# A product of zeros on TensorE ahead of each expert row of the last three tiles

## What is computed

```python
def expert_block(args):
    xi, ii, gi = args                              # 128 tokens, 128 experts each
    h = jnp.einsum('nhkd,nd->nhk', peer_u[ii], xi)
    a = jax.nn.gelu(h.astype(f32), approximate=False) * gi
    return jnp.einsum('nhk,nhkd->nd', a.astype(x.dtype), peer_v[ii])
```

## Time and profile before

| what | value |
|---|---|
| median of 3 runs | 2049.05 us |
| the profiled execution's own time | 2053.64 us |
| its span, first to last instruction | 2051.8 us |
| TensorE matmul busy, share of the span | 1600.6 us, 78% |
| GpSimd busy | 1224.8 us, 60% |
| VectorE busy | 1245.5 us, 61% |
| mean granted TensorE clock | 0.864 of full |
| moved by DMA | 675.08 MB, mean 329 GB/s |

### The profile page before, as it was taken

How to read it: one execution, slowest core, us unless ns; L and a number is a source line. 1 busy time by engine, 2 the same in 40 slices (tenths; PEclk the granted TensorE clock), 3 DMA queues, 4 the chain that set the end, 5 groups by cost and what they waited for, 6 DMA issues and landing times.

```text
span 2051.8 us, 16855 instructions
## 1 busy us (share of the span) xinstructions
PE 1600.6 (78%) x4837; PEld 798.0 (39%) x4837; DVE 1245.5 (61%) x3135; ACT 440.0 (21%) x1035; POOL 1224.8 (60%) x1370
## 2 busy tenths in 40 slices
PE   7988888879989897963758777758777757676867
PEld 6787464445444432411323323223332323222323
DVE  7821459878697776677857664455666436443534
ACT  2342112452333213111111111110212111111111
POOL 0181057755776666676666666666766665666663
PEclk9988989989999999986868798778887878778978
DMA  5453389987999999899899999999999998999996
GB/s 215 139 153 94 127 339 363 345 321 267 379 368 379 408 374 387 304 361 349 338 364 366 360 364 380 350 373 369 372 360 357 378 379 322 367 372 352 377 360 230
DMA packets 186699, 675.08 MB, mean 329 GB/s; under 512 B 20976, under 2 KB 23456, under 8 KB 186192
## 3 DMA queue, kind: packets, MB, share of 16 engines
q0 software_dynamic: 167056, 609.25, 78.6%
q1 hardware_dynamic: 17632, 59.51, 8.2%
q10 hardware_dynamic: 1920, 5.24, 0.7%
HBM read 669.71 MB, written 3.69 MB: 328 GB/s over the span
## 4 chain that ended last, share of the span: by engine, by line
PE 58%; issue 18%; DVE 10%; POOL 6%; DMA 5%; ACT 2%; another core or an unknown queue 2%; SPq 0%; DVEq 0%; ACTq 0%; POOLq 0%
PE bank L1035 40%; PE bank L930 2%; POOL region L693 2%; POOL region L680 2%; DMA wring<-in_pu,region 2%; PE first_banks L930 1%; PE bank L838 1%; DVE region L1510 1%; PE bank L734 1%; DMA small<-in_pv,region 1%; DVE region L1498 1%; DMA discretisation<-in_pv,region 1%; PE first_banks L987 1%; PE bank L987 1%
## 5 line engine op out<-in xcount | busy, mean ns | idle before, releaser
L1035 PE MATMUL bank<-region,small 128*128 128x512 f32 (+1 forms) x728 | 379.5, 658 | 124.7 <-issue 61.6
L693 POOL DMA_INDIRECT region<-in_pv,region x320 | 326.8, 1021 | 190.2 <-issue 80.8
L680 POOL DMA_INDIRECT region<-in_pu,region x298 | 310.2, 1041 | 162.2 <-issue 83.8
L1510 DVE CUSTOM_DVE_ANT_0 wring<-wring,first_banks 128x1024 f32<-128x1024 f32 x228 | 271.9, 1217 | 144.8 <-DMA wring<-in_pu,region 83.0
L680 POOL DMA_INDIRECT wring<-in_pu,region x278 | 270.2, 972 | 124.8 <-issue 77.1
L1035 PEld LDWEIGHTS bank<-region,small 128*128 128x128 f32 (+1 forms) x728 | 140.6, 198 | 337.3 <-issue 281.0
L1510 DVE CUSTOM_DVE_ANT_0 region<-region,first_banks 128x1024 f32<-128x1024 f32 x156 | 187.2, 1218 | 91.3 <-DMA region<-in_pu,region 66.8
L1035 PE MATMUL bank<-region 128*128 128x512 f32 x364 | 187.1, 648 | 54.8 <-issue 51.4
L1510 DVE CUSTOM_DVE_ANT_0 region<-region 128x1024 f32<-128x1024 f32 x142 | 171.7, 1224 | 45.0 <-DMA region<-in_pu,region 39.0
L1801 ACT ACTIVATE small<-small,region 128x128 f32<-128x128 f32 (+1 forms) x317 | 105.2, 385 | 314.7 <-issue 108.8
L1809 ACT ACTIVATE region<-region 128x4 f32<-128x4 f32 x144 | 29.3, 203 | 523.0 <-DVE region L1510 302.6
(11 more groups left out here) (371 smaller groups left out, 2410.9 us busy)
## 6 DMA issues: line engine op xcount, KB each, us to landing
wring<-in_w SPq DMA_DIRECT2D x100, 512.0 KB, 5.5
region<-in_pv,region POOLq DMA_INDIRECT x320
region<-in_pu,region POOLq DMA_INDIRECT x298
wring<-in_pu,region POOLq DMA_INDIRECT x278
region<-in_w SPq DMA_DIRECT2D x4, 512.0 KB, 4.9
small<-in_small ACTq DMA_DIRECT2D x1, 1669.0 KB, 9.0
xT<-in_xT SPq DMA_DIRECT2D x1, 1536.0 KB, 12.7
region<-in_x SPq DMA_DIRECT2D x3, 512.0 KB
```

The source lines that it names most:

```text
L680: pool.indirect_dma_start(ring_u[u_at.place[q]], None, io["pu"], bass.IndirectOffsetOnAxis(ind[:, k:k + 1], 0)).then_inc(g_u[u_at.place[q] ...
L693: pool.indirect_dma_start(ring_v[v_at.place[q]], None, io["pv"], bass.IndirectOffsetOnAxis(ind[:, k:k + 1], 0)).then_inc(g_v[v_at.place[q] ...
L1035: last = mm(bank[6 + hf][0:tn, :], diagonal[diag_at[d]][:, 0:tn], ring_v[v_at.place[q]][:, 512 * hf:512 * hf + 512], start=k == 0, stop=t ...
L1510: V.tensor_tensor_reduce(out=ring_u[u_at.place[q]], in0=ring_u[u_at.place[q]], in1=first_banks[:, :] if t > 1 else x1[t], scale=1.0, scala ...
```

## The change

In `weigh`, for every slot of the last three tiles but a tile's first, TensorE first adds the product of a 128x128 matrix of zeros with 256 columns of a constant to the sums in bank 6. It stands ahead of the waits for the slot's diagonal and for its V rows. The zeros are written once by ScalarE, in `do_banks(2)`, in the room of the sixteenth diagonal, so that the ring of diagonals shrinks from 16 to 15.

```diff
-DIAGS, LATE_DIAGS = 8, 16
+DIAGS, LATE_DIAGS = 8, 15
...
+        zeros = view(12928, 128)
...
+                    if t > 1 and k:
+                        if q == slot_base[2] + 1:
+                            pe.wait_ge(zeros_s, 1)
+                        mm(bank[6][0:tn, 0:256], zeros[:, 0:tn], s("k12")[:, 0:256], start=False, stop=False)
                     d = q - by_dve[q]
                     pe.wait_ge(diag_s, d + 1)
                     pe.wait_ge(g_v[v_at.place[q]], 16 * v_at.nth[q])
...
                 act.wait_ge(dots, slot_base[t])
+                if t == 2:
+                    S.activation(zeros, ident, ACT.Copy, scale=0.0).then_inc(zeros_s, 1)
```

More of the change, by code:

```diff
@@ L504, in hybrid_step @@
         x1_s = sem("x1_tile_ready")
-        x1_banks = sem("x1_tile_in_first_banks")
+        x1_banks, zeros_s = sem("x1_tile_in_first_banks"), sem("zeros_ready")
         sc_s, sce_s = sem("top_scores_ready"), sem("top_exponentials_ready")
```

## The result

The changed kernel takes **2074.73 us**, the median of 4 runs (2073.87 to 2080.42); the kernel before took 2049.17 us beside it (4 runs, 2047.36 to 2055.45). The ratio is 1.0125, with a 95% interval of 1.0097 to 1.0153: slower, by 25.6 us. The profiled execution is the slowest of the four, 2080.42 us with a span of 2078.6, which is 26.8 us more than the span before.

The account below looks back on a forecast made before the run. It took GpSimd's V gathers, held by TensorE's late reports, to bound the kernel. 2053.6 + 0.4 (writing zeros) + 45 (reports) = 2099 us profiled, so a median of 2095 us, 2.2% slower; range 2030 to 2150 us.

Parts of the forecast that it names:

- the 64: On TensorE: at most 64 loads and matmuls done but not reported, so 5.3 slots ahead and no longer 8.
- the crawl: TensorE's slow stretch after 32 matmuls at full pace: 2.8 us for each load and matmul, with a slot still unreported.
- The reports term, +45 us: GpSimd's V gathers wait for TensorE's late reports: 57 waits of 2.80 us, 160 us against 115.
- the shorter ring: ScalarE's diagonals, 15 places and not 16: taken at nothing, with 28 us left for the range.
- The main case: Reports limited by instructions, so GpSimd's V waits grow: 2095 us, own range 2065 to 2130 us, chance 0.60.
- The low clock is a result of the crawl: From 1003 to 2043 us TensorE isn't idle for lack of work; granted clock stays between 0.75 and 0.87.
- The clock's rival: Zeros keep TensorE's clock up, so GpSimd's V waits shrink: 1991 us for half, 1934 for all; chance 0.18.
- TensorE becomes the bound: Slots of 4.3 us at the low clock lose ground; up to 170 us show, 2150 to 2219 us; chance 0.08.
- hidden: Products hidden under GpSimd's 2.50 us a slot, V waits stay near 115 us: 2049 to 2058 us; chance 0.14.
- The crawl stands where DMA is saturated.: At 1040 to 1060 and 1740 to 1760 us: 407 and 409 GB/s with 7 and 8 matmuls.
- The 23 us: Delay of TensorE's increment after its work, for the `small` place that the gather at 1110.98 waited for.

Follow-up runs that it names:

- two products of 64 columns: Changed kernel with two products of zeros of 64 columns ahead of each row in place of one of 256: 2104.13 us, ratio 1.0259.
- half the products: Kernel before, without the second product (columns 512 to 1023) in all slots of the last three tiles but a tile's first and last: 2062.56 us, ratio 1.0037.
- ring of 15: Kernel before with 15 diagonals in place of 16 and no product of zeros: 2054.43 us, ratio 0.9993.
- pause of one column: Kernel before with a one-column GpSimd memset in each slot of the last three tiles: 2055.96 us, ratio 1.0017.
- ring of 16: Changed kernel with 16 diagonals again, the zeros lying in mask columns no longer needed: 2080.97 us, ratio 1.0124.
- no zeros at the end: Changed kernel without the products of zeros in the last 24 slots of the last tile: 2071.28 us, ratio 1.0090.
- 64 columns: Changed kernel with 64 columns in each product of zeros in place of 256: 2073.87 us, ratio 1.0085.
- 512 columns: Changed kernel with 512 columns in each product of zeros in place of 256: 2092.77 us, ratio 1.0211.
- zeros behind the waits: Changed kernel with the product of zeros after the waits for diagonal and V rows, on another chip: 1910.36 us, ratio 0.9990.
- pause of 128 columns: Kernel before with a 128-column GpSimd memset in each slot of the last three tiles, on another chip: 1913.91 us, ratio 1.0013.

## Why the prediction was right, and where it wasn't

**The direction and the 64: right, and shown.** The prediction took the zeros to be dear as instructions, since TensorE can be only 64 loads and matmuls ahead of its reports. The trace after counts 64 again in the crawl shown, in 5.3 slots where it was eight, and near 60 over all crawls; and two products of 64 columns cost twice what one of 256 does at the same slot duration. The Trainium skill's figure of 64 for TensorE's queue (page "TensorE: Matmul & The Clock Gate", its table of the engine) agrees with the count in the two crawls shown, and over all crawls it is met within some 10%.

**The reports term, +45 us: the step that failed.** The forecast, 2.2%, came out as 1.25%. It said "one wait for every 9.4 - 2.7 = 6.7 slots makes 384/6.7 = 57 waits", 160 us against 115. The length of one held: "remote" has 103.7/37 = 2.80 us again. The number didn't, nor did the sign named for it (50 to 70 waits, 140 to 190 us): 37 and not 57, and with those put down to a matmul 132.5 against 129.5 us. The term is 3 us in this profile, not 45. Three things were wrong in it, the least first. The 41 waits are from 1003 us on, by when 25 of the 384 V gathers had been issued, so it is one for every 359/41 = 8.8 slots and not 9.4. It let nothing else move when TensorE's unreported work shrinks, so that all 2.7 slots had to come out of V's 19 places. And it took V's waits to lie on the path at their full length, which the kernel with half the products refutes: there V's waits fall by 76 us, and the time doesn't follow. The reading that TensorE's reports are what GpSimd lacks was also only half of it, since VectorE's come late too.

**What was luck.** That the size came within reach of the forecast is in good part luck, for it rests on two costs that the sum doesn't have: the 22 us of the next paragraph stand where it had 45 us of V waits, of which 3 came. That the loads and matmuls are counted as instructions, and that the shorter ring costs nothing, was no luck. (The main case's upper bound of 2130 us is also some 8 us more than its terms give: 2049 + 0.4 + 73 = 2122.)

**What the time went into.** In the kernels of the first two groups without zeros (before, ring of 15, pause of one column) the three tiles take 1115.8 us in the mean and the tail 24.6 us. In the four with 12 instructions and 64 or 256 columns (changed, ring of 16, no zeros at the end, 64 columns) the three tiles take 1127.1, and the tail, without the one that has no zeros there, 35.4. That is 11.3 + 10.8 = 22 us, beside 25.6 us between the medians; the rest has no place. So:

- *The tail, about 11 us*, wasn't in my sum. TensorE has 12 slots left behind the last gather and no longer 7.5 to 10, and works each in 2.15 us and not 1.72. From the last V gather to the last slot's start it is 2067.45 - 2043.50 = 24.0 us. That this part is the zeros' is shown by the kernel without them at the end.
- *The three tiles, about 11 us* or 1% of them. No single wait carries it. VectorE's gated product, from 1003 us on and nearly all in tile 4, before: 78.2 + 26.5 = 104.7 us of waits in L1479; after: 97.3 + 44.5 = 141.8 us in L1484. Its waits for its own semaphore fall meanwhile, from 78 to 44 us. The U gathers wait 37.4 us for dot products and no longer 28.8. How these turn into 11 us is open.

**Why the backlog grows** I can argue, not show: TensorE may have 64 instructions unreported, so with 12 to the slot its work stands 2.7 slots nearer to its last report. If GpSimd follows the reports as before, the rest of its lead over TensorE grows by that much. 2.7 is about the difference in slots left (12.3 and 12.5 against 7.5 to 10). Where tile 3 ends the trace has both pictures: before, VectorE waited for a report 25 us after TensorE had begun its last slot; after, the last slot starts at 1717.23 and VectorE goes at 1719.15, having waited 28.3 us for work and not for a report. The work itself stood in a crawl for half of that time, from 1696.92 to 1710.91, so late reports are in both pictures: before at the tile's end, after in TensorE's own pauses.

```profile
1717.23 1.88 PE L1040 MATMUL bank<-region,small 128*128 128x512 f32 x4
...
1719.15 1.41 DVE L1540 SCALAR_TENSOR_TENSOR region<-region,bank 128x512 f32<-128x512 f32 x2 [28.29 <-PE bank L1040]
```

**"The low clock is a result of the crawl", so the clock stays.** The clock didn't stay within 0.75 to 0.87: it rose to 0.89. The crawl shrank, and the pauses before slots' matmuls with it, from 234.3 us in 192 to 95.9 + 54.9 = 150.8 us in 83 + 42 (L1040 and L1035). I had said that they stay. The slots before a crawl came out as said, five to six.

```profile
PE bank L1040 <- issue: 95.9, 83, 2.9
...
PE bank L1035 <- issue: 54.9, 42, 2.9
```

**The clock's rival fell all the same.** The change does what it is made for: some 160 us less at the low clock (395 to 235). Not one of them comes back as time. Over the kernels of the first chips the clock tells nothing of the time: 0.857 at 1.00, 0.901 at 1.0125, 0.935 at 1.021, 0.899 at 1.026, and with half the products 0.789 at 1.004. The Trainium skill's advice to leave no long idle gaps between bursts of matmuls (same page, section "Why this matters for your kernels") is about the clock, and the trace agrees that it rises when the gaps are filled. Read as advice on the time it fails here: in a stretch that waits for gathers nothing is bought with the clock.

**The rival "TensorE becomes the bound"** is what the tail is, in small, and what 512 columns make of it. **The rival "hidden"** had the waits right (near 115 us) and the time wrong on the first chips; on the other chip the times are as it says, though there no V gather waits at all.

**"The crawl stands where DMA is saturated."** In the two stretches of the kernel before it does. In the same two stretches after:

```profile
1040.00:1060.00 20.00, 2.93 (x8) 1.99 (x7) 9.89 (x20) 2.38 (x8) 12.57 (x14) 0.52 1.03 410
...
1740.00:1760.00 20.00, 13.58 (x35) 6.50 (x34) 10.03 (x19) 1.80 (x6) 15.12 (x17) 0.85 1.03 410
```

410 GB/s in both, with 8 matmuls in one and 35 in the other. And on the other chip DMA stays at 403 and 405 GB/s for 900 us, and no V gather waits. Full DMA alone doesn't make the reports late. The 23 us are not the most either. The `region` place that this gather of the kernel before writes was read last by matmuls that were through at about 1729.8, so the report came 38 us late:

```profile
1724.53 5.31 PE L1035 MATMUL bank<-region 128*128 128x512 f32 x12
...
1767.61 0.95 POOL L693 DMA_INDIRECT region<-in_pv,region  x1 [4.15 <-remote]
```

What makes the reports late on the first chips is open, for VectorE's as for TensorE's; whether the recording of the trace has a part in it is untested too. So is why a tile takes some 372 us there with three quite different loads on TensorE (a third of "three tiles": 371.9 us before, 374.2 after, 376.0 with half the products) and 324 to 334 us on the other chip (zeros behind the waits, pause of 128 columns). The runs in which the chip changed couldn't settle it, since none of them repeats a kernel of the first chips.

## What to carry to other kernels

Filling a waiting engine with dummy work isn't free even where the row says "idle": each instruction takes a place among the some 60 that TensorE could have unreported here, and behind the last transfer every one of them is plain length. If filling is tried at all, use few and long products, leave them out where the work ends, and judge by the time, not by the clock. Before a wait is priced at its length, ask who would wait if it went: halving the products here moved the wait from one ring of buffers to the other and won nothing. When one engine's reports look late, look at another engine's waits for itself before you blame the first. And time a small effect beside its base on the same chip: two chips differed by 137 us for one kernel, and the cost of 1.25% on one kind did not show on the other, where the zeros stood behind the waits or beside a pause.

## What the runs showed of the hardware

- The same kernel takes 2049 to 2056 us on some chips and 1912 us on another. The kernel before has no trace from there, but near relatives do (zeros behind the waits, pause of 128 columns): their three tiles take 978 and 996 us against 1111 to 1121 in the kernels without zeros on the first chips, and DMA moves 405 and 403 GB/s against 360.
- TensorE's semaphore increments came up to 38 us after the matmul on the first chips, and TensorE slowed to one load and matmul in 1.4 to 2.8 us once some 60 were unreported. Late ones come together: where tile 3 of the kernel before ends, five are recorded from 1701.62 to 1701.86. On the other chip, in the last three tiles, each increment on record stands within 0.02 us of its matmul's modelled end.
- VectorE's increments were late on the first chips as well: its waits for its own semaphore took up to 9.6 us (half the products, at 1143), and none over 0.04 us on the other chip.
- GpSimd's gap of 0.30 us between two gathers hides a write of one column (0.12 us) entirely; one of 256 columns (0.33 us) adds 0.19 us to the slot.
